# Sample key products moved from GpSimd to VectorE in a hybrid decoder step

## What is computed

```
k_past = cache_k[page_table]          # 8 samples x 512 past tokens x 8 heads x 128
v_past = cache_v[page_table]
s_past = einsum('bqhmd,bkhmd->bhmqk', q, k_past)     # m: two maps of 64 dims in a head
p  = softmax(concat([s_past, s_new]) * DA_SCALE)
pd = p[:, :, 0] - lam * p[:, :, 1]
o  = einsum('bhqk,bkhe->bqhe', pd[..., :P], v_past) + einsum('bhqk,bkhe->bqhe', pd[..., P:], v)
```

## Time and profile before

| what | value |
|---|---|
| median of 3 runs | 2157.49 us (2157.33 to 2158.73) |
| profiled execution | 2158.41 us, span 2156.6 us |
| TensorE busy | 2022.6 us, 94% of the span |
| VectorE, ScalarE, GpSimd busy | 810.4, 645.5, 792.2 us |
| mean granted TensorE clock | 0.964 |

### The profile page before, as it was taken

How to read it: one execution, slowest core, us unless ns; L and a number is a source line. 1 busy time by engine, 2 the same in 40 slices (tenths; PEclk the granted TensorE clock), 3 DMA queues, 4 the chain that set the end, 5 groups by cost and what they waited for, 6 DMA issues and landing times.

```text
span 2156.6 us, 38506 instructions
## 1 busy us (share of the span) xinstructions
PE 2022.6 (94%) x15037; PEld 1862.3 (86%) x15037; DVE 810.4 (38%) x1418; ACT 645.5 (30%) x1158; POOL 792.2 (37%) x353
## 2 busy tenths in 40 slices
PE   6998998899989997999889999999999999989995
PEld 5987998798879896999779878987997799779995
DVE  4354336525542554200361444054416322550005
ACT  5122222222212222312242333333324332442222
POOL 2353326234523432454453213322341233115453
PEclk9999999999999998999999999999999999989998
DMA  6644333424443353532234342434244324433322
GB/s 183 190 131 131 99 118 113 138 82 118 133 118 91 113 148 89 160 90 87 73 102 118 115 151 79 118 118 157 69 118 138 125 81 136 154 135 113 94 79 79
DMA packets 357437, 252.55 MB, mean 117 GB/s; under 512 B 15136, under 2 KB 324785, under 8 KB 356721
## 3 DMA queue, kind: packets, MB, share of 16 engines
q1 hardware_dynamic: 316364, 186.75, 30.2%
q10 hardware_dynamic: 40900, 63.41, 8.6%
HBM read 213.61 MB, written 36.96 MB: 116 GB/s over the span
## 4 chain that ended last, share of the span: by engine, by line
PE 68%; issue 11%; POOL 7%; SPq 4%; DVE 4%; DMA 3%; ACT 2%; POOLq 0%; ACTq 0%; DVEq 0%
PE proj L989 55%; PE scratch L989 8%; POOL wlo L554 4%; PE score L989 3%; DMA qb<-q_sample_rows 2%; SPq L466 2%; SPq L458 2%; POOL mix L601 1%; PE scratch L992 1%; POOL kv L575 1%; DVE probw L1519 1%; POOL mix L615 1%; DVE xlo L1367 0%; DMA kv<-in_cache_v 0%; DVE ek L1750 0%
## 5 line engine op out<-in xcount | busy, mean ns | idle before, releaser
L989 PE MATMUL proj<-xhi,wlo 128*128 128x268 f32 x4128 | 1205.4, 292 | 21.4 <-DVE xlo L1369 10.4
L989 PE MATMUL proj<-xlo,whi 128*128 128x268 f32 x4128 | 1192.4, 289 | 0.0
L989 PE MATMUL proj<-xhi,whi 128*128 128x268 f32 x4128 | 1191.9, 289 | 0.0
L554 POOL TENSOR_TENSOR wlo<-wraw,whi 128x1024 fp32r<-128x1024 f32 x258 | 626.9, 2439 | 1048.8 <-ACT whi L626 1048.6
L989 PEld LDWEIGHTS proj<-xhi,wlo 128*128 128x128 f32 x4128 | 789.0, 191 | 48.6 <-issue 22.1
L989 PEld LDWEIGHTS proj<-xlo,whi 128*128 128x128 f32 x4128 | 788.1, 191 | 1.1
L989 PEld LDWEIGHTS proj<-xhi,whi 128*128 128x128 f32 x4128 | 785.3, 190 | 0.0
L626 ACT ACTIVATE whi<-wraw 128x1024 fp32r<-128x1024 f32 x258 | 265.2, 1047 | 448.1 <-PE proj L989 287.5
L1356 DVE TENSOR_TENSOR tz<-proj,rstd 128x536 f32<-128x536 f32 x72 | 51.5, 716 | 330.2 <-PE proj L989 329.8
L1666 DVE TENSOR_SCALAR mix<-proj,cols 128x536 f32 x32 | 24.8, 776 | 341.4 <-ACT te L632 178.5
L575 POOL TENSOR_TENSOR kv<-kv,qb 128x1024 f32<-128x1024 f32 x32 | 78.7, 2465 | 109.1 <-DMA qb<-q_sample_rows 57.2
(11 more groups left out here) (258 smaller groups left out, 1780.1 us busy)
## 6 DMA issues: line engine op xcount, KB each, us to landing
wraw<-in_w_in SPq DMA_DIRECT2D x192, 512.0 KB, 4.0
wraw<-in_w_out SPq DMA_DIRECT2D x64, 512.0 KB, 4.0
kv<-in_cache_k SPq DMA_DIRECT2D x128, 128.0 KB, 2.3
kv<-in_cache_v SPq DMA_DIRECT2D x128, 128.0 KB, 2.3
sst<-in_state_gla ACTq DMA_DIRECT2D x32, 512.0 KB, 4.8
out<-sst ACTq DMA_DIRECT2D x32, 512.0 KB, 3.3
hbuf<-h_residual ACTq DMA_DIRECT2D x2, 4288.0 KB, 15.1
vb<-v_sample_rows ACTq DMA_DIRECT2D x32, 256.0 KB, 5.5
```

Of the source, the lines that this page charges most:

```text
L554: pool.tensor_tensor(wlo[:, slot, :, 0:width], wraw[:, kc, :, 0:width], whi[:, slot, :, 0:width].bitcast(F32), ALU.subtract).then_inc(s_lo, 1)
L989: return pe.matmul(out, lhsT, rhs, start=start, stop=stop, skip_group_check=True)
```

## The change

VectorE does the product of a sample itself, directly ahead of its sum, and takes over the two waits for the fetched keys and the query. GpSimd is left with the weight subtractions in the pair stage. The list of products is dropped; the list of sums is changed: sample 1 alone in step 12, samples 2 and 3 in step 13.

```diff
-KEY_PRODUCT = {11: [0], 12: [1, 2], 13: [3], 14: [4, 5], 15: [6, 7]}
-KEY_SUM = {11: [0], 12: [1, 2], 13: [3], 14: [4, 5], 15: [6, 7]}
+KEY_SUM = {11: [0], 12: [1], 13: [2, 3], 14: [4, 5], 15: [6, 7]}
...
             def pair(g):
                 for s in range(24):
-                    for b in KEY_PRODUCT.get(s, ()):
-                        pool.wait_ge(s_kv[b % KB], 256 * g + 64 * (b // KB + 1))
-                        pool.wait_ge(s_qb[b % KB], 32 * g + 16 * (b // KB + 1))
-                        pool.tensor_tensor(kv[b % KB][:], kv[b % KB][:], qb[b % KB][:, None, :].to_broadcast([P, NPG, 2 * P]),
-                                           ALU.mult).then_inc(s_prod, 1)
                     lo(24 * g + s + 2, (s + 2) % 4)
...
                 def key_sums(b):
+                    dve.wait_ge(s_kv[b % KB], 256 * g + 64 * (b // KB + 1))
+                    dve.wait_ge(s_qb[b % KB], 32 * g + 16 * (b // KB + 1))
+                    dve.tensor_tensor(kv[b % KB][:], kv[b % KB][:], qb[b % KB][:, None, :].to_broadcast([P, NPG, 2 * P]),
+                                      ALU.mult).then_inc(s_prod, 1)
                     dve.wait_ge(s_prod, 8 * g + b + 1)
                     dve.tensor_reduce(sall[:, :, 4 * b:4 * b + 4], kv[b % KB][:].rearrange("p k (m d) -> p k m d", d=64),
                                       AX.X, ALU.add).then_inc(s_kred, 1)
```

## The result

The changed kernel takes 2119.22 us in the median of 4 runs (2115.73 to 2122.08), the kernel before 2157.41 (4 runs, 2154.81 to 2158.73): a ratio of 0.9823, 95% interval 0.9808 to 0.9837. That is 38.2 us less; 2121 with a range of 2106 to 2149 was forecast. The profiled execution took 2118.19 us (span 2116.4, mean granted clock 0.969 where it was 0.964), 40.2 less than that of before.

What follows compares the result with a forecast made beforehand. TensorE is busy 94% of the span, so only its idle time and slow clock can be won. 22.0 + 22.2 + 1.7 - 9.6 = 36.3 us off the profiled 2158.4 gives 2122.1, median 2121; range 2106 to 2149.

Steps and rivals of the forecast that it cites:

- The mechanism: Pair 1: every late step leads back to a sample product on GpSimd; rival 1, 2121 us, chance 0.46.
- The product, 1.26 us: On VectorE, one sample's product takes 1.26 us; with its sum of 1.21, 2.47 a sample.
- one or two a pair: Sign: products on VectorE of 1.2 to 1.3 us, one or two a pair stretched to 2.5 to 3.7.
- Step 12 to `ST`, 22 us: Steps 12 to 16: `ST` runs at 362.2 instead of 367.7, gaining 5.5 us a pair, 22 in all.
- The `pd` wait: Step 12, `PT3A`: wait and slow stretch behind it go, TensorE comes out earlier by 4.5 + 2.9 = 7.4 us.
- VectorE would sit out subtraction 18: Step 15: VectorE sits out this GpSimd subtraction once, 2.4 us; `ST` waits 3.2 us instead of 1.7.
- the keys themselves are no limit: Steps 13 to 16: keys 5 to 7 go out near 355 and land ahead of 358.
- `V1`, 22.2 us: Step 21: earlier load 19 removes all 17.1 us of waits for values; `V1` itself shortens, 5.1 more.
- The rival that SyncE's reads and issues set the values' time: `V1` waits as now because of SyncE's own 18.6 us, not load 19: 2134 us, chance 0.17.
- `SD`, a loss of 9.6 us: Step 18: with earlier loads all pairs wait like pair 0, 1.50 us plus 1.7 lost at half clock; 3 x 3.2.
- 22.2 + 1.7 - 9.6 = 14.3: Terms from `ST` on: `V1` gain 22.2, pair 3's fifth `pd` wait gone 1.7, `SD` loss 9.6 us.
- The rival on the other side: Steps 13 to 15: VectorE becomes what TensorE waits for, products at 2.40 us meeting subtractions: 2177 us, chance 0.10.

Runs made afterwards that it cites:

- Experiment 1: Changed kernel with GpSimd's waits for keys and query put back at their old steps, without the products: 2137.50 us.
- experiment 2: Kernel before with each step's weight subtraction placed ahead of that step's products, all products staying on GpSimd: 2123.88 us.
- Experiments 6 and 8: 6: changed kernel, GpSimd's step 18 subtraction waits for the samples' softmax: 2112.73 us. 8: kernel before, subtractions ahead of products, same wait: 2118.27 us.
- experiment 4: Changed kernel with every key sum done twice on VectorE: 2155.06 us; then with products on one page of four only: 2110.86 us.
- the halves: The change for samples 0 to 3 alone, GpSimd keeping the other products: 2148.63 us; for samples 4 to 7 alone: 2145.77 us.

## Why the prediction was right

**The mechanism.** It said that every late step leads back to sample products on GpSimd, by what stands behind their waits. Experiment 1 shows this for half of the gain and experiment 2 from the other side. What experiment 1 leaves out is the products' own time in GpSimd's queue, 2.4 us each ahead of the same subtractions. By experiment 2, which keeps the products but behind the subtractions and has 32 of the 38 us, most of that too is order. Experiments 6 and 8 leave some 5 us to the move itself; no run takes it apart further.

**The product, 1.26 us:** 1.21 to 1.23 where nothing meets it. Product 2, in step 13, was stretched in every pair (2.27 to 2.44), and product 7 in pair 0 (2.17): "one or two a pair", as the prediction's sign had it, but a little shorter than its 2.5 to 3.7. The sum had not counted one in step 13; it had one in step 15, which came in pair 0 alone.

**Step 12 to `ST`, 22 us.** From the copy of step 10 that ScalarE makes (`vtok`) to `ST` took 56.70, 58.08, 57.90, 56.13 us in the four pairs, and now 50.77, 51.32, 50.77, 50.75: 25.2 less. The `pd` wait went as worked out, the own-key product with its 2.60 us included. What failed is the step at `ST`: that VectorE would sit out subtraction 18, and that "the keys themselves are no limit". ScalarE's rounding of that chunk waited for its load:

```profile
345.07 1.06 ACT L620 ACTIVATE whi<-wraw 128x1024 fp32r<-128x1024 f32 x1 [1.63 <-DMA wraw<-in_w_in]
```

So the subtraction came at 346.20, behind the start of product 6, and product 7 then waited for keys, 1.42, 0.81 and 0.70 us in pairs 1 to 3. `ST` waited 2.0 us a pair instead of 3.2. The keys came about when they were forecast: "ahead of 358", less the 9.4 us by which this pair now starts sooner (its `vtok` copy at 300.3 instead of 309.7), is 348.6, and product 7 began at 348.98. They were no limit only as long as the subtraction stood in front of them. The prediction had called it a sign of being wrong if VectorE's wait for keys reached TensorE: it does here, by about a microsecond in three pairs.

**`V1`, 22.2 us:** all four waits are gone and all four `V1` take 1.93. The rival that SyncE's reads and issues set the values' time is refuted; load 19 was the key, as the four pairs of experiment 1 show, though it is only 4.3 us ahead of `ST` and not 7.

**`SD`, a loss of 9.6 us.** The wait came in all four pairs, 1.45 to 1.49 us where 1.50 was said. The stretch at half clock behind it did not come in pair 1; why is not shown, since pairs 2 and 3 have it although they, like pair 1, have a stretch behind `ST` as well. Windows of after, first behind `ST` in pair 1 and then behind `SD` in pairs 0, 2 and 3 (the fields of the earlier trace rows):

```profile
352.50:355.90 3.40, 3.40 (x17) 3.40 (x16) 2.93 (x6) 1.28 (x3) 2.04 (x1) 0.51 0.24 77
178.40:181.80 3.40, 3.40 (x18) 3.40 (x17) 3.22 (x6) 0.95 (x2) 2.37 (x1) 0.50 0.05 14
...
567.50:570.90 3.40, 3.40 (x17) 3.40 (x17) 3.24 (x6) 0.94 (x1) 2.39 (x1) 0.50 0.12 34
765.80:769.20 3.40, 3.40 (x18) 3.40 (x18) 3.26 (x6) 0.85 (x1) 2.48 (x1) 0.55 0.25 73
```

Pair 0 had its wait and its stretch before the change too. So pairs 1 to 3 lost 3 x 1.5, and pairs 2 and 3 a stretch of 3.4 at half clock each, 2 x 1.7: 7.9 us instead of 9.6. The stretches behind `ST` itself were in no term of the sum: two pairs had one before (0 and 1), three have one now (1 to 3). From `ST` to `PO` in step 22 the pairs took 58.97, 62.73, 64.50, 68.69 and now 56.25, 57.88, 61.00, 62.32: 17.4 less, where 22.2 + 1.7 - 9.6 = 14.3 was said. With the 25.2 these are 42.6, of which the profiled execution keeps 40.2. Of the 2.4 lost elsewhere, 1.6 lie between `PO` of pair 1 and the copy of pair 2. There `PO` waits a little longer than before, and runs at half clock behind that wait (granted 0.50 in 411.40 to 412.80), as it did not before; `PO` of pair 1 in after and in before:

```profile
409.49 3.00 PE L983 MATMUL scratch<-ub,pw 128*128 128x268 f32 x8 [1.50 <-DVE oT L1475]
...
430.46 2.07 PE L989 MATMUL scratch<-ub,pw 128*128 128x268 f32 x8 [1.11 <-DVE oT L1481]
```

**Luck.** Over the four pairs, the way from the copy to `ST` and the way from `ST` to `PO` each gained 3 us more than was said, and the profiled execution came out 3.9 us under its forecast (2118.2 for 2122.1). The median is only 1.8 under: the forecast took the median to lie 0.9 below the profiled execution, and here it lies 1.0 above.

**The rule against it.** The Trainium skill, SBUF — State Buffer, section Who interferes with whom, says that of two such instructions (VectorE's with two inputs in SBUF, GpSimd's that reads SBUF) the later is blocked until the earlier has ended. The trace agrees: the product of 362.51 in experiment 4 ends 1.08 us after the subtraction that it met (361.90 + 2.84 = 364.74). The same section says that a reduction on this chip never meets GpSimd; the sums kept 1.22 us throughout, beside subtractions too (346.33 against 346.20 above).

**The rival on the other side,** VectorE as the bound, did not come. It takes 9.8 us more of VectorE's work a pair, and the collisions that come with it, to lose the gain: experiment 4 has the time of before, and is no slower.

## What to carry to other kernels

Ahead of moving work off an engine that is mostly idle, look at what stands in its queue behind the work's waits: here one line's place gave 32 of 38 us, and with one added wait the kernel that moves nothing has the time of the changed one; the move itself was worth some 5 us. A receiving engine with 39% busy time can still have no room in the steps that matter; put work in and take work out to see it. When two steps of a chain are late, mending one may win little, since the other eats the lead: 7.5 and 10.3 us for the halves, 38 for both.

## What the runs showed that I had not expected

Small differences in the order of two engines decide over 2 us. Product 6 takes 1.23 us if it starts 1.1 us ahead of subtraction 18 and 3.31 if it starts 0.6 behind it, and the last softmax instruction 0.22 us if it is first and 2.30 if it starts 0.14 behind subtraction 20. Where VectorE is first, GpSimd pays less: a subtraction of 2.40 us took 2.65 and 2.72 in the rows above and 2.93 in the earlier trace rows. Runs of one kernel on one chip differ by several microseconds, 2120.49 to 2132.85 in experiment 2, 2149.05 to 2162.06 in 13 runs of before beside experiment 4. That such races are the reason is likely, but was not tried by itself.
